# Next weights split in halves during three attentions, and the value rows' weights loaded in one piece with the last group's factors made earlier

## What is computed

```python
y = h @ w_qkv
q = rmsnorm(y[..., :D_MODEL].reshape(bsz, t, n_kv, N_HEADS // n_kv, HEAD_DIM), g_q)
kv = y[..., D_MODEL:]
k = rmsnorm(kv[..., :kv_w].reshape(bsz, t, n_kv, HEAD_DIM), g_k)
v = kv[..., kv_w:].reshape(bsz, t, n_kv, HEAD_DIM)
...
q = apply_rope(q, cos, sin)
k = apply_rope(k, cos, sin)
o = sliding_window_attention(q, k, v, k_c, v_c, sink)
x = x + gt1 * (o @ w_out)
```

## Time and profile before

| | |
|---|---|
| median of 3 runs | 3861.72 us (3858.34 to 3864.71) |
| the profiled execution's own time | 3865.26 us |
| its span in the profile | 3863.5 us |
| busy in it: PE, DVE, ACT, POOL | 3621.7, 2644.5, 1413.4, 1418.6 us |

### The profile page before, as it was taken

The page is one execution under the profiler, slowest core; times in us unless marked ns, Lnnn a source line. Parts: engine busy times, 40 slices in busy tenths (PEclk is TensorE's granted clock), DMA queues, the critical chain, the costliest instruction groups (busy, mean ns, idle before and its releaser), DMA issues. The chain is left out here.

```text
span 3863.5 us, 55647 instructions
## 1 busy us (share of the span) xinstructions
PE 3621.7 (94%) x18886; PEld 2938.5 (76%) x18886; DVE 2644.5 (68%) x5198; ACT 1413.4 (37%) x2036; POOL 1418.6 (37%) x602
## 2 busy tenths in 40 slices
PE   8878999999999999999998988889998988979999
PEld 5746787788888788888887766678887877667877
DVE  7654899988888699999998656575445026745440
ACT  2443133345545323332333247532223133744331
POOL 3013344333333344444442236432222322443443
PEclk9978999999999999999999999999999999999999
DMA  6403444335545755555545470231111214032222
GB/s 211 141 12 125 151 146 140 126 128 193 191 152 194 254 191 194 195 194 190 190 154 170 129 158 12 72 109 60 65 60 45 66 61 130 1 120 87 92 80 89
DMA packets 249026, 490.54 MB, mean 127 GB/s; under 512 B 49187, under 2 KB 126499, under 8 KB 244044
## 3 DMA queue, kind: packets, MB, share of 16 engines
q1 hardware_dynamic: 228236, 447.95, 35.5%
q10 hardware_dynamic: 20672, 41.07, 2.9%
HBM read 411.59 MB, written 73.68 MB: 126 GB/s over the span
## 5 line engine op out<-in xcount | busy, mean ns | idle before, releaser
L426 POOL TENSOR_TENSOR ahead_low<-w_raw,ahead_high 128x1024 fp32r<-128x1024 f32 (+1 forms) x159 | 428.1, 2692 | 885.2 <-ACT ahead_high L362 885.2
L229 PE MATMUL psum<-h_high,ahead_high 128*128 128x512 f32 (+1 forms) x1504 | 540.8, 360 | 1.4 <-POOL ahead_low L426 1.4
L230 PE MATMUL psum<-h_low,ahead_high 128*128 128x512 f32 (+1 forms) x1504 | 537.4, 357 | 0.0
L231 PE MATMUL psum<-h_high,ahead_low 128*128 128x512 f32 (+1 forms) x1504 | 535.7, 356 | 0.0
L1932 POOL TENSOR_TENSOR pick_u_low<-pick_u_raw,pick_u_high 128x1024 fp32r<-128x1024 f32 x128 | 309.7, 2419 | 559.0 <-ACT pick_u_high L2009 559.0
L1796 POOL TENSOR_TENSOR v_low<-v_raw,v_high 128x1024 fp32r<-128x1024 f32 x128 | 334.2, 2632 | 368.8 <-ACT v_high L1793 368.8
L362 ACT ACTIVATE ahead_high<-w_raw 128x1024 fp32r<-128x1024 f32 (+1 forms) x159 | 178.0, 1119 | 741.7 <-PE psum L231 712.3
L229 PE MATMUL psum<-h_high,pick_u_high 128*128 128x512 f32 x1024 | 414.3, 405 | 1.9 <-POOL pick_u_low L1932 1.9
L229 PE MATMUL psum<-a_high,v_high 128*128 128x512 f32 x1024 | 399.2, 390 | 9.0 <-DVE a_low L2254 9.0
L230 PE MATMUL psum<-h_low,pick_u_high 128*128 128x512 f32 x1024 | 404.6, 395 | 0.0
L231 PE MATMUL psum<-h_high,pick_u_low 128*128 128x512 f32 x1024 | 401.6, 392 | 0.0
(11 more groups left out here) (395 smaller groups left out, 7266.2 us busy)
## 6 DMA issues: line engine op xcount, KB each, us to landing
pick_u_raw<-in_expert_uT SPq DMA_DIRECT2D x128, 512.0 KB, 3.5
v_raw<-in_expert_v SPq DMA_DIRECT2D x128, 512.0 KB, 4.9
mod_w<-in_w_mod SPq DMA_DIRECT2D x88, 512.0 KB, 3.9
w_raw<-in_ffn_up SPq DMA_DIRECT2D x84, 512.0 KB, 3.5
gelu_dram<-pick_gelu ACTq DMA_DIRECT2D x128, 256.0 KB, 2.0
gates_dram<-gate_plane SPq DMA_DIRECT2D x32, 1024.0 KB, 7.4
p<-gelu_dram SPq DMA_DIRECT2D x128, 256.0 KB, 5.0
g<-gates_dram SPq DMA_DIRECT2D x64, 512.0 KB, 4.4
```

Source lines behind the costliest of these rows:

```text
L229: nc.tensor.matmul(bank, w_high, x_high, start=first, stop=False)
L230: nc.tensor.matmul(bank, w_high, x_low, start=False, stop=False)
L231: return nc.tensor.matmul(bank, w_low, x_high, start=False, stop=last)
L426: nc.gpsimd.tensor_tensor(w_low[r % 2][:, :, :], raw[r % n_raw][:, :, :], w_high[r % 2][:, :, :].bitcast(F32), ALU.subtract).then_inc(k.w_ ...
```

## The change

1. `Ahead` can split a weight block in `pieces`; the three attentions use 2. In step `first` of `then_at` ACT rounds the first half block and in step `first + 1` the second; POOL subtracts them in steps `first + 1` and `first + 2`, after it has scaled half 1 of that step.
2. The block of the products loads all of the rows' weights (1 MB in one transfer) instead of half; the four transfers in the rows' block are gone.
3. In the rows' block the squares of group 2 are summed on PE before the first step, the mean stands in DVE's step 0 (was 1), the root in ACT's step 0 (was 1), the refining in DVE's step 1 (was 2). ACT's four swap transfers of chunk 11 move from step 0 to step 1. SP spreads group 1 at step 0 (was 3). `root` waits until the previous group's factors have left their tile.

```diff
+    def round(self, act, r, i=0):
+        s = self.piece(i)
         act.wait_ge(self.loaded[r].sem, self.at[0][r] + 16)
...
+        self.nc.scalar.activation(self.high[r][:, s, :], self.raw[r][:, s, :], ACT.Copy).then_inc(self.rounded.sem, 1)
+    def subtract(self, pool, r, i=0):
+        s = self.piece(i)
+        pool.wait_ge(self.rounded.sem, self.at[1] + (r - self.first) * self.pieces + i + 1)
...
-                if w in then_at:
-                    then.subtract(pool, then_at.index(w))
+                for r, first in enumerate(then_at):
+                    if first < w <= first + then.pieces:
+                        then.subtract(pool, r, w - first - 1)
...
-                if w in then_at:
-                    then.round(act, then_at.index(w))
+                for r, first in enumerate(then_at):
+                    if first <= w < first + then.pieces:
+                        then.round(act, r, w - first)
...
+            if loaded:
+                for x in beside:
+                    x.tensor_first(pe)
...
+        if g:
+            act.wait_ge(self.y_out.sem, self.y_out.at(16 * g))
...
-                sp.wait_ge(k.w_low.sem, k.w_low.at(2 * RING + 1))
-                sp.dma_start(self.rows_raw[:, :], self.t["swa_v"][0][:, 0:D]).then_inc(self.rows_in.sem, 16)
+                sp.wait_ge(k.w_low.sem, k.w_low.at(2 * RING + 2))
+                sp.dma_start(self.rows_raw[:, :], self.t["swa_v"][0]).then_inc(self.rows_in.sem, 16)
...
     def sync(self, sp, s):
-        if s == RING - 1:
+        if s == 0:
             self.spread(sp, 1)
...
         if s == 0:
+            self.root(act, 2)
+        if s == 1:
             self.swap(act, self.n - 1)
-        if s == 1:
-            self.root(act, 2)
+
+    def tensor_first(self, pe):
+        self.sum(pe, 2)
...
         if s == 0:
+            self.mean(dve, 2)
             self.rotate(dve, 10)
         if s == 1:
-            self.mean(dve, 2)
-        if s == 2:
             self.refine(dve, 2)
```

More of the change, by code:

```diff
@@ L234, with __init__ @@
 class Ahead:
-    def __init__(self, k, w, k_chunks, raw_at, split_at, parts=1, left=None, last=False, exact=False):
+    def __init__(self, k, w, k_chunks, raw_at, split_at, parts=1, left=None, last=False, exact=False, pieces=1):
         k.names += 1
+        self.pieces = pieces
         self.k, self.nc, self.w, self.parts, self.kp, self.split_at = k, k.nc, w, parts, k_chunks // parts, split_at
@@ L256, in __init__ @@
         self.at = [s.base for s in self.loaded], self.rounded.base, self.ready.base
-        for s, n in [(s, 16) for s in self.loaded] + [(s, self.n - self.first) for s in (self.rounded, self.ready)]:
+        for s, n in [(s, 16) for s in self.loaded] + [(s, (self.n - self.first) * pieces) for s in (self.rounded, self.ready)]:
             s.base += n
@@ L267, in load, with piece @@
             sp.dma_start(self.raw[r][:, :, :], source).then_inc(self.loaded[r].sem, 16)
-    def round(self, act, r):
+    def piece(self, i):
+        return slice(i * self.kp // self.pieces, (i + 1) * self.kp // self.pieces)
+    def round(self, act, r, i=0):
+        s = self.piece(i)
         act.wait_ge(self.loaded[r].sem, self.at[0][r] + 16)
[L271 to L275, removed]
+        self.nc.scalar.activation(self.high[r][:, s, :], self.raw[r][:, s, :], ACT.Copy).then_inc(self.rounded.sem, 1)
+    def subtract(self, pool, r, i=0):
+        s = self.piece(i)
+        pool.wait_ge(self.rounded.sem, self.at[1] + (r - self.first) * self.pieces + i + 1)
+        self.nc.gpsimd.tensor_tensor(self.low[r][:, s, :], self.raw[r][:, s, :], self.high[r][:, s, :].bitcast(F32), ALU.subtract
                                      ).then_inc(self.ready.sem, 1)
     def wait(self, pool):
-        pool.wait_ge(self.ready.sem, self.at[2] + self.n - self.first)
+        pool.wait_ge(self.ready.sem, self.at[2] + (self.n - self.first) * self.pieces)
     def wait_exact(self, pe):
@@ L727, with stage_rows @@
 LOW_LEAD = 2
-def stage_rows(k, w, n_blocks, width, tiles, out, at, beside=(), n_banks=8, step=BANK, loaded=None, loaded_raw=None):
-    n_loaded, lead = (RING, LOW_LEAD) if loaded else (0, 0)
+def stage_rows(k, w, n_blocks, width, tiles, out, at, beside=(), n_banks=8, step=BANK, loaded=None, loaded_raw=()):
+    n_loaded, lead = len(loaded_raw), LOW_LEAD if loaded else 0
     nc = k.nc
@@ L740, in stage_rows @@
     assert width <= step
-    raw = [loaded_raw[:, r * step:(r + 1) * step] if loaded else k.place(f"rows_w{k.names}_{r}", at + r * step, step) for r in range(RING)]
+    ring = [k.place(f"rows_w{k.names}_{r}", at + r * step, step) for r in range(RING)]
+    raw = lambda s: loaded_raw[s] if s < n_loaded else ring[s % RING][:, 0:width]
     high, low = ([k.place(f"rows_{s}{k.names}_{r}", at + (RING * i + r) * step, step, dtype=FR) for r in range(RING)]
@@ L750, in _ @@
             for s, (b, c) in enumerate(steps):
-                if s >= RING:
-                    sp.wait_ge(k.w_low.sem, k.w_low.at(s - RING + 1))
                 if s >= n_loaded:
-                    sp.dma_start(raw[s % RING][:, 0:width], w[b][:, c * width:(c + 1) * width]).then_inc(k.weights_in[s % RING].sem, 16)
+                    if s >= n_loaded + RING:
+                        sp.wait_ge(k.w_low.sem, k.w_low.at(s - RING + 1))
+                    sp.dma_start(raw(s), w[b][:, c * width:(c + 1) * width]).then_inc(k.weights_in[s % RING].sem, 16)
                 for x in beside:
@@ L775, in round_rows @@
                     act.wait_ge(k.product_done.sem, k.product_done.at((s - RING + 1) * tiles))
-                nc.scalar.activation(high[s % RING][:, 0:width], raw[s % RING][:, 0:width], ACT.Copy).then_inc(k.w_high.sem, 1)
+                nc.scalar.activation(high[s % RING][:, 0:width], raw(s), ACT.Copy).then_inc(k.w_high.sem, 1)
             for s in range(RING - 1):
@@ L795, in subtract_rows @@
                 dve.wait_ge(k.w_high.sem, k.w_high.at(s + 1))
-                nc.vector.tensor_tensor(low[s % RING][:, 0:width], raw[s % RING][:, 0:width], high[s % RING][:, 0:width].bitcast(F32), ALU.subtract
+                nc.vector.tensor_tensor(low[s % RING][:, 0:width], raw(s), high[s % RING][:, 0:width].bitcast(F32), ALU.subtract
                                         ).then_inc(k.w_low.sem, 1)
@@ L1640, in stage_dilated @@
                               [(f.mixT[:, 4 + g, :], k.psum[:, 6 + g % 2, :])] if i == TILES - 1 else ()))
-    ahead = Ahead(k, t["w_out"], KD, 48000, W_OUT_SPLIT)
+    ahead = Ahead(k, t["w_out"], KD, 48000, W_OUT_SPLIT, pieces=2)
     stage_attention(k, "dil", pairs, [37000 + i * TOK for i in range(6)], FIRST_ROWS_AT, PICKS_AT, ahead, (8, 12))
@@ L2415, in na_layer @@
                               at_tile, 2 * (g - 1) + (1 if latent else 2) if g and i in (0, TILES) else 0, stores, heads_masked=2 * (g + 1) if i == 0 else 0))
-    ahead = Ahead(k, t["na_o"], KD, FREE + RING * D, NA_O_SPLIT)
+    ahead = Ahead(k, t["na_o"], KD, FREE + RING * D, NA_O_SPLIT, pieces=2)
     behind = FREE + NA_HEADS * (RPB_H + 1) * GRID_W
@@ L2463, in __init__ @@
         self.rope_in, self.rows_in = k.shared("table_in"), k.shared("rows_ahead_in")
-        self.rows_raw = k.place("swa_rows_ahead", SWA_AT, D)
+        self.rows_raw = k.place("swa_rows_ahead", SWA_AT, 2 * D)
         self.swap_in = [k.shared(f"chunk_in{r}") for r in range(GROUP)]
@@ L2702, in scalar @@
         if s == 0:
+            self.root(act, 2)
+        if s == 1:
             self.swap(act, self.n - 1)
-        if s == 1:
-            self.root(act, 2)
+    def tensor_first(self, pe):
+        self.sum(pe, 2)
     def tensor(self, pe, s):
-        if s == 0:
-            self.sum(pe, 2)
+        pass
     def vector(self, dve, s):
         if s == 0:
+            self.mean(dve, 2)
             self.rotate(dve, 10)
         if s == 1:
-            self.mean(dve, 2)
-        if s == 2:
             self.refine(dve, 2)
@@ L2745, in swa_layer @@
     rotary.products()
-    stage_rows(k, t["swa_v"], 1, SWA_WIDTH, ALL_TILES, lambda n, i: [(v[:, i, :], 0, SWA_WIDTH)], SWA_AT, (rotary,), 6, SWA_WIDTH, rotary.rows_in, rotary.rows_raw)
+    stage_rows(k, t["swa_v"], 1, SWA_WIDTH, ALL_TILES, lambda n, i: [(v[:, i, :], 0, SWA_WIDTH)], SWA_AT + D, (rotary,), 6, SWA_WIDTH, rotary.rows_in,
+               [rotary.rows_raw[:, c * SWA_WIDTH:(c + 1) * SWA_WIDTH] for c in range(KD)])
     per = 2
@@ L2760, in swa_layer @@
                                   sinks=(2 * q, 2 * q + 1)))
-    ahead = Ahead(k, t["swa_o"], KD, H_LOW, SWA_O_SPLIT)
+    ahead = Ahead(k, t["swa_o"], KD, H_LOW, SWA_O_SPLIT, pieces=2)
     stage_attention(k, "swa", pairs, [FREE + i * TOK for i in range(6)], FREE + 6 * TOK, PICKS_AT, ahead, (24, 28), sink=k.par("sink", 0, NA_HEADS))
```

## The result

| kernel | median, us (lowest to highest, runs) | ratio to before [95% interval] |
|---|---|---|
| before | 3860.03 (3857.09 to 3864.71, 4) | |
| after | 3832.34 (3828.57 to 3833.88, 4) | 0.9926 [0.9908, 0.9943] |

What follows compares the result with a forecast made beforehand. PE, busy nearly throughout, was held to wait on POOL's late scalings and the rows' block's end. Attentions 25.9 (30.4 less 4.5) plus rows' block 3.4 gave 29.3 us: 3836.0 profiled, 3832.4 median; range 3824 to 3847.

Steps and rivals of the forecast that it cites:

- What a split costs: Attentions: a whole block's split loses 5.52 us in swa, 5.55 dilated, 4.14 in na; 30.4 for six, 25.9 regained.
- ACT's share: Attentions: a half's rounding ahead of an ACT copy moves PE by 0.5 us; 9 halves, 4.5 us (bounds 0 and 6).
- PE loses what POOL is late beyond 2.24 us: Attention model, read in swa: POOL's scaling leads PE's turn by 2.24 us, and only lateness beyond that costs PE.
- a half's 1.35 us: swa: with halves, the scaling of step 26 would start 1.35 us late, under 2.24, so POOL's loss goes to zero.
- the lead: swa step 21: POOL is done 2.24 us before PE turns; rival that it doesn't hold, 12 us back, 14%.
- the 5.52 us: swa: four POOL steps take 20.74 us with a whole block's split against 15.22 without, the loss per split.
- POOL's waits: Attentions: POOL's 6.7 us waits on ACT's rounding would shrink to about 0.5 to 2 us, 12 times.
- DVE is blocked: Rival, attentions: POOL's half subtractions hold DVE through the shared port, 0.6 us each, 7 us, giving 3839; 12%.
- the order that the prediction named: Attentions: ACT's rounding ends with a step's second exponentials, when DVE is past half 0 scaling and reads PSUM next; cost zero.
- The rows' block: Without the load wait, factors leave near 3256.7 instead of 3263.34; gain 3.4 us, bounds 1.9 and 5.0.
- The slots: Rows' block: next late link, group 1's scaling behind chunk 11's rotation and swap; SP spreads at 3263.4 instead of 3266.79.

Runs made afterwards that it cites:

- the table's kernels: Kernels whose stage lengths were compared: before, after, the change repeated, and variants changing the halves, POOL's subtraction steps or the swap; rows' block 20.2 to 26.2 us.
- after once more: The changed kernel, unaltered, measured again beside the last version on the same chip: 3835.89 us, ratio to before 0.9936.
- halves alone: The three attentions' half-block splits of the change, with the rows' block of the kernel before: 3836.58 us, ratio to before 0.9937.

## Why the prediction was right, and where it wasn't

- **The forecast**, 3832.4, came within 0.1 us of the median. So close a hit is luck: the four runs alone spread over 5.3 us, the profiled execution was forecast at 3836.0 and took 3832.6, and the change measured again fell 24.2 us where 29.3 was the sum. What holds beyond luck is the cause: POOL's long waits on ACT's rounding are gone, PE's waits on POOL with them, and the stages shrank by what was forecast.
- **What a split costs** held, 26.0 us of stages against 25.9. By attention it was off both ways: swa gave 9.9 where 11.04 less 2.0 for ACT was forecast, na 7.4 of 8.28 less ACT's share, and the dilated one 8.8, or 5.4 in the execution with the longer stretch at 1.2 GHz, of 11.1 less ACT's share.
- **"PE loses what POOL is late beyond 2.24 us"** is the step that failed, though the forecast didn't hang on it: a half's 1.35 us was inside the lead either way. It priced whole blocks moved a step at 11 us; they cost 400.6 - 394.4 = 6.2 (394.4 is the sum of the three stages before less 30.4), the halves 4.4. In swa, where it was followed turn by turn, the lateness of ACT and that of POOL don't add: the larger decides. And behind the waits of 2.71 and 4.76 us stood a stretch at a lower clock, which the 5.52 us had in it unseen. The model met PE's longest wait of 4.8 us, which is why it looked sound, but not the loss of 5.52.
- **The halving** was read as a cause beside the move. It is worth at most 2 us in the stages (400.6 against 398.8, more than half of it in the dilated one with its scatter) and can't be told in the time; the move carries the rest, and without it the halves cost 12 us more than whole blocks (436.9 against 424.8).
- **POOL's waits** of 0.5 to 2 us: 1.15 to 2.3 in swa and the dilated one, in na 3.65 for the first half, where a scaling of 256 columns stands ahead, and 0.61 for the second. **ACT's share** grew by 9.1 us in its rows, not 4 to 6. Some of that is no new loss: in swa the 0.20 and 0.59 us of the earlier trace rows had gone into the long wait of each split block and are back, and all halves together cost the stages 4.4.
- **DVE is blocked**: not in the changed kernel's swa, where its scaling of half 0 took 486 ns (512 columns) and 554 ns (640) in the median, as before, and none took over 0.6 us. The rival was real all the same: with POOL later it came true, as the last section shows. What kept it out is the order that the prediction named.
- **The rows' block**: forecast 3.4. The first pair of profiles gave 4.3; the means over the table's kernels, those with another place for the swap left out, give 25.8 - 22.3 = 3.5. The slots were next, as forecast, behind the swap that the change itself moves: the last spread started 12.7 us after the first rounding, where 13.9 was forecast, and undoing that move gave the block 1.7 more.

## What to carry over

When one engine waits for another's side work, first ask whether the instruction can stand one step later in the waiting engine's list; cutting it in pieces comes after, and alone it doubled the number of waits here. Where two engines are late for a third, try the larger lateness as the price before their sum, and add what the clock costs after a long wait. When a chain is shortened, look at what was moved out of its way: here the swap became the last link, and the block was shorter with it in front.

## What the runs showed of the hardware

The length of the dilated stage differed between executions of the same instructions, 57.8 to 61.2 us, and the granted clock with it (0.82 and 0.72). In swa the clock fell to 1.2 GHz for a few us behind PE's waits of 2.7 and 4.8 us, and not behind those of 1.15. Behind the wait of 2.17 us it fell in two executions (the two kernels with the swap elsewhere) and not in three (after, after once more, halves alone).

A scaling on DVE from SBUF to SBUF was held by an instruction on POOL, while reads of PSUM were not. In na, after:

```profile
2414.75 2.20 POOL L1496 TENSOR_SCALAR na_scores<-na_scores,na_stat 128x768 f32<-128x768 f32 x1
...
2416.28 1.08 DVE L1554 TENSOR_SCALAR na_scores<-na_scores,na_stat 128x768 f32<-128x768 f32 x1
```

It takes 0.62 us in the median; here it ended 0.41 us after POOL's, as in the earlier trace rows. A weight subtraction does the same. In swa, with whole blocks a step later and subtracted twice:

```profile
3378.24 2.35 POOL L287 TENSOR_TENSOR ahead_low<-ahead_raw,ahead_high 128x1024 fp32r<-128x1024 f32 x1
3379.35 1.53 DVE L1559 TENSOR_SCALAR swa_scores<-swa_scores,swa_stat 128x512 f32<-128x512 f32 x1
```

This scaling takes 0.49 us elsewhere and ended 0.29 us after POOL's subtraction. With the swa attention of the change DVE's reduction of 256 columns from PSUM, started 0.03 us into POOL's subtraction, took its usual 0.47 us:

```profile
3355.73 0.47 DVE L1576 TENSOR_SCALAR_CACHE_REDUCE swa_scores<-psum,swa_stat 128x256 f32<-128x256 f32 x1
```

The Trainium skill (SBUF — State Buffer, "Who interferes with whom") has an exclusive lock on a port pair of SBUF that the two engines share, and names DVE's tensor_scalar among what can take it; the rows here agree with it.
